# A two-layer hybrid decoder step on one core: layers written out without a barrier, row projections first on unscaled x, final norm at the copy

## The reference, cut to what matters

```
per layer:
  h = RMSNorm(x); P = h @ w_in           # q/f/i/out-gate of HGRN2, q of NSA, compressed/selected/window K and V,
                                         # branch gates (24 columns), two merge gates
  a = HGRN2(h)                           # 4 heads, gated linear attention in chunks of 64
  b = NSA(h)                             # compressed-block + selected-block + window attention, 8 heads of 64
  x += (sigmoid(g_a) * (a W_a) + sigmoid(g_b) * (b W_b)) @ w_out
  h2 = RMSNorm(x)
  x += W_down( gelu(causal_depthwise_conv3(h2 W_gate)) * (h2 W_up) )     # d_ff 2816
y = RMSNorm_final(x)
rmsnorm(x, g) = x * rsqrt(mean(x*x) + 1e-6) * g
```

## Time and profile before

| | us |
|---|---|
| median of 3 runs (1240.15 to 1241.97) | 1241.48 |
| the profiled execution | 1239.53 |
| its span on the core | 1237.8 |
| TensorE busy in it | 1190.6 |
| VectorE / ScalarE / GpSimd busy | 647.3 / 485.5 / 152.7 |
| mean granted clock of TensorE | 0.989 |

### The profile page before, as it was taken

The page is one execution under the profiler, slowest core; times in us unless marked ns, Lnnn a source line. Parts: engine busy times, 40 slices in busy tenths (PEclk is TensorE's granted clock), DMA queues, the critical chain, the costliest instruction groups (busy, mean ns, idle before and its releaser), DMA issues.

```text
span 1237.8 us, 20578 instructions
## 1 busy us (share of the span) xinstructions
PE 1190.6 (96%) x8397; PEld 1010.8 (82%) x8397; DVE 647.3 (52%) x1256; ACT 485.5 (39%) x800; POOL 152.7 (12%) x290
## 2 busy tenths in 40 slices
PE   5999999999999999999889999999999999999995
PEld 3785656778999999999868575667799999999994
DVE  3244254448566777754232524544575577776433
ACT  2130245454355555532122213654534555454220
POOL 0035110003120100100002440000211110100000
PEclk9999999999999999999989999999999999999998
DMA  8453242047844445334524354223495444532501
GB/s 262 136 162 142 71 139 85 25 131 214 266 136 137 137 142 170 107 111 134 174 59 149 103 175 128 69 69 103 130 277 181 137 137 157 168 118 86 194 1 42
DMA packets 136669, 166.01 MB, mean 134 GB/s; under 512 B 14612, under 2 KB 97334, under 8 KB 136246
## 3 DMA queue, kind: packets, MB, share of 16 engines
q1 hardware_dynamic: 136570, 164.64, 41.9%
HBM read 156.22 MB, written 12.46 MB: 136 GB/s over the span
## 4 chain that ended last, share of the span: by engine, by line
PE 90%; DVE 5%; ACT 2%; issue 1%; DMA 0%; SPq 0%; POOLq 0%; DVEq 0%; PEldq 0%; ACTq 0%
PE mm L639 63%; PE ax L639 23%; PE ax L642 4%; DVE ring_low L1854 1%; ACT mixb L1240 1%; ACT work_parts L1240 1%; DMA attb<-in_norm_final 0%; DVE mixb L1669 0%; ACT L1240 0%; ACT work L1240 0%; DVE hT L1553 0%; DVE xT L2011 0%; DVE mixb L2024 0%; DVE work L1750 0%; DVE mixb L1889 0%
## 5 line engine op out<-in xcount | busy, mean ns | idle before, releaser
L1854 DVE TENSOR_TENSOR ring_low<-ring,work_parts 128x2048 fp32r<-128x2048 f32 (+1 forms) x96 | 206.9, 2155 | 124.8 <-ACT work_parts L1240 115.5
L639 PE MATMUL mm<-h_low,work_parts 128*128 128x320 f32 x832 | 259.0, 311 | 0.0
L639 PE MATMUL mm<-work_parts 128*128 128x320 f32 x832 | 257.2, 309 | 0.9 <-DVE ring_low L1854 0.9
L639 PE MATMUL mm<-work_parts,ring_low 128*128 128x320 f32 x832 | 256.0, 308 | 0.0
L1240 ACT ACTIVATE work_parts<-ring 128x2048 fp32r<-128x2048 f32 (+1 forms) x96 | 173.7, 1810 | 154.0 <-PE ax L639 78.3
L639 PE MATMUL mm<-hT,ring 128*128 128x320 f32 (+1 forms) x896 | 213.3, 434 | 0.7 <-DVE hT L1553 0.7
L639 PEld LDWEIGHTS mm<-hT,ring 128*128 128x128 f32 (+1 forms) x896 | 144.3, 175 | 58.0 <-issue 2.2
L639 PEld LDWEIGHTS mm<-work_parts 128*128 128x128 f32 x832 | 156.1, 188 | 3.9 <-issue 2.0
L639 PEld LDWEIGHTS mm<-work_parts,ring_low 128*128 128x128 f32 x832 | 156.4, 188 | 0.0
L639 PEld LDWEIGHTS mm<-h_low,work_parts 128*128 128x128 f32 x832 | 156.2, 188 | 0.2
L639 PE MATMUL ax<-act_parts,work_parts 128*128 128x320 f32 x544 | 125.8, 310 | 2.3 <-DVE ring_low L1854 1.6
(11 more groups left out here) (214 smaller groups left out, 1440.6 us busy)
## 6 DMA issues: line engine op xcount, KB each, us to landing
ring<-in_w_gate_up SPq DMA_DIRECT2D x44, 1024.0 KB, 6.5
ring<-in_w_in SPq DMA_DIRECT2D x12, 2048.0 KB, 8.4
ring<-in_w_in SPq DMA_DIRECT2D x18, 1024.0 KB, 7.9
ring<-in_w_down SPq DMA_DIRECT2D x6, 1536.0 KB, 6.7
ring<-in_w_out SPq DMA_DIRECT2D x4, 2048.0 KB, 13.6
ring<-in_w_down SPq DMA_DIRECT2D x4, 2048.0 KB, 8.6
ring<-in_w_down SPq DMA_DIRECT2D x4, 1280.0 KB, 5.9
ring<-in_cache_cmp_kv SPq DMA_DIRECT2D x32, 128.0 KB
```

Of the source, the lines that this page charges most:

```text
L639: return nc.tensor.matmul(out, lhsT, rhs, start=start, stop=stop)
L1854: V.tensor_tensor(unit_of(u, ring_r), unit_of(u, ring), unit_high(u).bitcast(F32), ALU.subtract).then_inc(*st.up(w_low))
```

## The change

- The loop over the layers is gone: each engine's program has both layers written out, each layer with semaphores of its own (`mm_full[L]` and so on), and `depart`, `clear` and `arrived` are gone. The bank lists of a layer follow on those of the one before (`Banks.before`).
- hT is first x times gain. `compressed_rows` leads the layer on it, k outermost, with three banks open; `norm1_sums` stands between k = 3 and k = 4. Five one-column products turn rs into columns (`rs_columns`), by which ACT scales kvc at its copy. Then DVE multiplies hT by rs, and hf0 waits for these.
- Parameters of the next layer are turned ahead of the last unit but one of w_down; the last unit goes output by output; x's last tiles and their h follow one by one, squares by ACT tile by tile.
- The final norm is a sum per token (24 products of one column), applied as h is copied from PSUM, half by ACT, half by DVE; the store is in three DMAs.
- Order: kvn goes with levels 0 to 2, nq with 3 to 5, level 6 behind the compressor, whose banks hidk and hidv move ahead of lv6. DVE multiplies all four rotated q by sine first. ACT and DVE empty the turned tiles of unit 2 before exponentials and gate 3.

```diff
-BLOCKS = (["par", "w_hf", "w_hq", "w_kvc", "cmp", ...
+BLOCKS = (["par", "w_kvc", "w_hf", "w_hq", "cmp", ...
...
-    out = [("par", "V"), ("norm1", "A"), ("cst", "V")]
+    out = [("norm1", "A"), ("rst", "V"), ("cst", "V")]
...
     for kk in range(3, len(LEVELS)):
+        if kk == len(LEVELS) - 1:
+            out += [("hidk", "A"), ("hidv", "A")]
         out += level_plan(kk)
-    out += [("hidk", "A"), ("hidv", "A"), ("kt0", "A"), ("kt1", "V")]
+    out += [("kt0", "A"), ("kt1", "V")]
...
+            def compressed_rows(l):
+                pe.wait_ge(*landed_at("w_kvc", l))
+                w = kt_of("w_kvc", KD, 280)
+                banks = [begin(MM[L], f"kvc{i}") for i in range(3)]
+                for k in range(KD):
+                    if k == KD // 2:
+                        norm1_sums()
+                    pe.wait_ge(h_ready[L], k + 1)
+                    for i in range(3):
+                        lhs = hT[:, k, i:SEQ:2] if i < 2 else hT[:, k, SEQ:T]
+                        n = 256 if i < 2 else 280
+                        last = mm(banks[i][0:TM[i], 0:n], lhs, w[:, k, 0:n], k == 0, i == 2 and k == KD - 1)
+                        if i < 2:
+                            last = mm(banks[i][0:TM[i], 256:280], hT[:, k, P * i:P * i + TM[i]], w[:, k, 256:280], False,
+                                      k == KD - 1)
...
+            def rs_columns():
+                bank = begin(AXR[L], "rst")
+                pe.wait_ge(rs_ready[L], 1)
+                for c, toks in enumerate(RS_COLUMNS):
+                    last = mm(bank[0:TM[2] if c == 2 else P, c:c + 1], rs[:, toks], ident[:, 0:1], True, True)
...
-            with pe.Fori(0, DEPTH) as l:
+            for l in range(DEPTH):
                 layer(l)
-                depart(pe, l + 1)
+            bank = begin(END_AX, "sums")
             for k in range(KD):
+                pe.wait_ge(end_sq, k + 1)
+                for i in (0, 2, 1):
+                    last = mm(bank[0:TM[i], i:i + 1], sq[:, k, P * i:P * i + TM[i]], ones[:, 0:1], k == 0 and i == 0,
+                              i == 1 and k == KD - 1)
+                if k == 3:
+                    outputs_turned_back(0)
+            last.then_inc(end_rs, 1)
+            outputs_turned_back(1)
...
                 out_gate(2)
+                turned(2)
                 unit_exp(3)
                 out_gate(3)
-                turned(2)
...
+                for k in range(KD):
+                    if k < KD - 1:
+                        ve.wait_ge(kvc_read[L], k + 1)
+                    else:
+                        ve.wait_ge(*MM[L].filled("kvc2"))
+                    V.tensor_tensor(hT[:, k, :], hT[:, k, :], rs[:, 0:T], ALU.mult).then_inc(*st.up(h_ready[L]))
...
                 for m in range(4):
                     bank = take(AXR[L], f"nqr{m}")
                     V.tensor_tensor(qT[:, m, :], bank[:, 0:T], con("sinq"), ALU.mult).then_inc(*st.up(ax_dve[L]))
+                for m in range(4):
                     link(V.tensor_tensor(qraw[:, m, :], qraw[:, m, :], con("cosq"), ALU.mult))
...
                 for m in range(4):
                     bank = take(AXR[L], f"dn1_{m}")
                     V.tensor_tensor(xT[:, 4 + m, :], xT[:, 4 + m, :], bank[:, 0:T], ALU.add).then_inc(*st.up(x_ready[L]))
+                    ve.wait_ge(*st.settled())
+                    ve.sem_inc(*st.up(ax_dve[L]))
+                    gained(4 + m, gain, entered())
```

## The result

The changed kernel takes 1224.46 us, median of 5 executions (1222.72 to 1228.13); the kernel before took 1240.26 beside it (1239.72 to 1241.97). The ratio is 0.9871, 95% interval 0.9853 to 0.9889. Forecast were 1218.5 us and a range of 1214.5 to 1225. So sign and range held, the range by 0.5 us; the gain is 15.8 us where 23 were put. The profiled execution took 1222.72, with a span of 1220.9.

A forecast was written before the change was run, and what follows sets the result against it. TensorE, busy 96% of 1237.8 us, was taken as the bound. Gains 10.3 + 2.6 + 8.3 + 2 x 0.8 + 2 x 0.3 = 23.4 us gave 1218.1, put at 1218.5; range 1214.5 to 1225.

The forecast's parts named there:

- rival (1): Slow clock at hi1 stays, further falls at new weak stretches, each 1.5 to 2 us: 1221 to 1226; chance 0.22.
- signs of being wrong: Issue gap inside a layer, windows at 0.50 anywhere but start and tail, or DVE's multiplies making hf0 wait.
- The sum: Whole kernel: all gains add to 23.4 us, giving 1218.1 as median, put at 1218.5.
- Between the layers: From layer 0's last product to hf0: 17.6 us shrink to 7.3 apart from kvc, gain 10.3 (9.0 to 11.2).
- They only move: Row projections kvc, 14.4 us, go from behind hq to the layer's head at the same price.
- The start: Before layer 0's hf0: hf0 at 41.9 against 44.5, 2.4 us lost to low clock, gain 2.6 (1.5 to 3.4).
- The end: Behind the last product: 23.4 us become 15.1, gain 8.3, small sums at 0.23 each; 5 at halved clock.
- Queries and compressor: Per layer: vc1 and vc2 waits save 1.0, new kt1 wait costs 1.5, hi1's clock gives 1.3; net +0.8.
- The rule on the clock: Skill page: clock halves behind idle stretches, so gaps of 0.5 us before hi1 did not do it; trace disagrees.
- Turned tiles first: Unit 2's tiles emptied before exponentials: tpc2's 2.33 us wait goes, skt0_3 waits instead; gain 0.3 us per layer.
- Levels: Levels 4 and 5 with one query tile between: cover holds by 0.7, kt0 loses 0 to 0.5 us, taken as 0.
- rival (3): Straight-line code lets TensorE run dry, about 5 us each time; slower than before, 1242 to 1250; chance 0.02.

The follow-up runs named there:

- bank-by-bank run: Changed kernel with kt1 behind hi0, conv states before kvc's second half, Exp table early, plus kvc bank by bank within each half: 1213.75 us, ratio 0.9779.
- run with both edits: Changed kernel with kt1 transposes issued behind hi0 and conv-state transposes ahead of the second half of kvc: 1215.69 us, ratio 0.9813.
- first try at the start: Changed kernel with ten dummy products of 320 columns on constant data before x arrives: 1222.49 us, ratio 0.9855.

## Why the prediction was right, and where it was not

**The number.** Sign and range held, but the median of 1224.5 lies outside the band of the forecast itself (1216 to 1221) and in that of rival (1), 1221 to 1226. That rival's mechanism is only half of what happened: the fall at hi1 did not stay, others came. And one of the prediction's own signs of being wrong was seen: windows at 0.50 inside a layer. Without gains in the layers that no step had ("The sum", at the end of this section), the time would have been above the range, and that is luck.

**Between the layers: the plan was right, one price was not.** Forecast was a gain of 10.3 us; it is 8.9. No gap is left, kvc follows the last product directly, sums 4.4, columns 1.3, conv states 1.46: 7.2 us, where 7.0 stood without the parameters (their 0.3 now stands ahead of the last product). What failed is "They only move", said of kvc's 14.4 us. The same products cost 8.08 + 8.08 = 16.2, because the change also turned the order from bank by bank to all banks for each k. The bank-by-bank run gives 14.7. Why the other order costs TensorE 0.2 us per k, and whether it is the bank itself, is not shown.

**The start: mechanism right, two terms short.** kvc began at 18.16, where 18.1 was put. Forecast hf0 at 41.9, measured 45.1. The price of kvc is 1.8 of this. The rest is the clock: 2.4 us were put for its low part, by the sums of before, but the first half of kvc took 11.7 - 8.1 = 3.6 too long. In the seven traces that have the same instructions up to there, that half took 9.9 to 14.1 us (9.2 to 16 with the two other orders of kvc), so the start alone spreads the time by several us. One execution of before could not show this spread. Of the 5.4 us between the changed kernel's executions the start can be only a part: the slowest has a mean granted clock of 0.986, the two fastest 0.993, and this mean leaves the start out.

**The end.** Forecast 15.1 us behind the last product, measured 17.0. The small sum at 0.23 was sized well ((1206.62 - 1203.74) / 12 = 0.24). But in this execution the clock fell in the tail: the first half was turned in 2.6 us instead of 1.4, the second twelve sums took 3.2 instead of 2.9. In the run with both edits, where the clock held until the sums were done, the same tail takes 15.4 (1196.82 to 1212.2). The prediction had the low clock here as a bound of 3 us and took the other end. The traces with this order of the tail fill the whole of that bound: four have 15.4 us, three 17.0, one 17.4, and two, low almost throughout, 18.4.

**Queries and compressor: three terms as forecast, one not thought of.** kt1 waits 1.54 and 1.40 us for ACT's Gelu (forecast 1.5), the waits ahead of vc1 and vc2 are gone, hi1 is at 7.0 in both layers. Only the worth of those waits was put low: with the fall taken out, the stretch from hi0 to hi1 is 1.4 and 1.6 us shorter, where 1.0 stood. What rival (1) said came at other places, two of the three that it named (the stretch of rs columns and conv states, and the kt1 wait): hf0 and hi0 of layer 0 lost 1.7 us each to the clock, within its 1.5 to 2 for each further fall.

**The rule on the clock.** In the first try at the start TensorE stood idle for 1.08 us and the clock went to 0.50; with the wait filled it did not. The Trainium skill, page "TensorE: Matmul & The Clock Gate", Part 1, ties the fall to an idle stretch; the start agrees with it in that a wait stood ahead of the fall. The rows at hf0 do not agree with it: TensorE was busy all through 40 to 46 us and the clock fell at 46, behind one-column products and 16-column transposes.

Three places can be counted over the traces of the changed kernel and of the twelve experiments, two layers each. At hf0, with one-column products and transposes together ahead of it (four traces), the clock fell in 6 of 8 layers; with the two apart (nine traces), in none of 18. At hi0, behind the kt1 wait (four traces), it fell in 4 of 8; with no such wait (nine), in none of 18. In or just behind the 15-column products that follow hi1, it fell in none of 8 layers of the traces with the kt1 wait and in 4 of 18 of those without it, with at most 0.1 us idle in the 2 us around it. So both edits took away what they aimed at, a wait is not needed for a fall, and a fall that is gone can come back at a later weak stretch, less often. What decides whether a given weak stretch loses the clock stays open.

My own reading, that the two gaps of 0.5 us made hi1 slow, is not borne out: with the gaps back, hi1 kept its clock in the profiled execution. Why the kernel before lost it there in both layers is therefore not shown. The same page of the Trainium skill calls the onset of the full clock variable between executions of one kernel. No kernel here has two traces; in seven that are alike up to there the first half of kvc took 9.9 to 14.1 us, which agrees.

**Turned tiles first: right.** tpc2 no longer waits (2.33 before), skt0_3 waits 1.74 in its place, the table load stands behind the copies: "the stall moves, it does not go". With 0.6 us the gain per layer is twice the 0.3 that was put.

**Levels and code.** No level waits, and no gap by issue comes inside a layer, so rival (3) did not happen. A gap put down to issue, 0.78 us at 283 us and 0.66 at 884 in the kernel before, is gone as well; it was in no step of mine, and what ended it was not tried.

**The sum.** Boundary -1.4, start -3.2, end -1.9 against the forecast; the layers in between brought 2.2, the forecast's own 2.2, but only because 3.4 us of falls are made up by as much gain that had no step or more than its step: 1.8 at the two gaps put down to issue (from start to start), 1.0 from hi0 to hi1, 0.6 from the tiles. What else there is, a few tenths either way (hi1 itself, kt1, the parameters ahead of the last product), cancels.

## What to carry to other kernels

Where one engine is busy 98% of the time, what is left lies in its clock and in the order of its own work: ask of each stretch of narrow products whether it can be cut in two or put between dense ones, and of each wait what dense work can go ahead of it. Then look at the next weak stretch, for a fall can show up there. When products are moved, keep their order of banks as well, or price the new order. And fill an idle start with products that nobody needs, up to the first real one: it was worth 8.3 us in the medians here (4.3 and 8.0 by the stages), against some 2 us when one wait of 1 us was left open.

## What the runs showed of the hardware

- The granted clock reads 1.00 from the beginning of each execution's trace, but the transposes of x took 7.4 us in all kernels with an idle start and 4.6 behind ten dummy products. Ahead of its first change the column can read 1.00 while the lengths show half rate: go by the lengths.
- By the lengths, in the ten traces without added products the clock rose between about 22 and 38 us, though TensorE was busy from 9 us on with one gap of 1 us.
- The two falls in the changed kernel's layers cost 1.7 us each in dense work (8.83 us for 7.13 at hi0, 36.41 for 34.72 at hf and hq), one with a wait ahead of it and one without.
- With 128x128 weights a product of one column costs 0.22 to 0.26 us, a 16-column transpose 0.07, and twelve 128-column transposes 1.4 us at full clock and 2.6 at half.
- 20 products of kvc over three banks cost 7.3 us bank by bank, 8.1 with the bank changed after each pair, 8.4 with the two products of 24 columns last in each k.
- A load of ACT's table took 1.28 us and the next exponential began 0.02 us behind it; put into ACT's idle time it took 1.4 us off the wait at skt0_3 (1.76 to 0.34), though no time was gained in the medians.
